# Two blocks of transformer layers on one core: other places for latents, forget steps, taps and first norms, a halved sub-norm reciprocal, and squares summed by TensorE

## The reference

```
first network                                      second network (twice)
h += attention(rms_norm(h))  # layer 0             y = rms_norm(x) @ w_in  -> four branches
h += conv_ffn(rms_norm(h))                          a: chunk band attention, 4 heads, relative bias
h += recurrent_mixer(rms_norm(h))  # layer 1        b: latents: rms_norm of 256 and 128 columns, up-projected
h += conv_ffn(rms_norm(h))                             to 4 heads, rotary part, chunk causal attention
attention: 8 heads of dilated mixture,              c: 4 heads, causal, logits + cumulated log forget gates
  and 4 differential heads:                         d: u = value * sigmoid(gate); causal depthwise convolution
  o = (softmax_1 - lam * softmax_2) @ v                over 31 taps; layer norm; silu
  o = rms_norm(o, b_sub_norm) * 0.8                x += sum_n(sigmoid(gate_n) * (branch_n @ w_branch_n)) @ w_o
                                                   x += relu(rms_norm(x) @ w_up)^2 @ w_down
                                                   at the end: rms_norm(x)
```

## Time and profile before

| | us |
|---|---|
| median of three runs | 2975.66 |
| the profiled execution, its own time | 2974.41 |
| its span | 2972.6 |
| PE busy | 2828.2 (95%) |
| DVE busy | 1354.6 (46%) |
| ACT busy | 1209.6 (41%) |
| POOL busy | 1244.1 (42%) |
| mean granted TensorE clock | 0.976 of full |

### The profile page before, as it was taken

How to read it: one execution, slowest core, us unless ns; L and a number is a source line. 1 busy time by engine, 2 the same in 40 slices (tenths; PEclk the granted TensorE clock), 3 DMA queues, 4 the chain that set the end, 5 groups by cost and what they waited for, 6 DMA issues and landing times.

```text
span 2972.6 us, 32386 instructions
## 1 busy us (share of the span) xinstructions
PE 2828.2 (95%) x12934; PEld 2286.1 (77%) x12934; DVE 1354.6 (46%) x2094; ACT 1209.6 (41%) x1781; POOL 1244.1 (42%) x550
## 2 busy tenths in 40 slices
PE   8998999999879999997899999999978999999997
PEld 7775788888757888875677788888756777888886
DVE  4565651545875415436456552022245566531113
ACT  3554442444544424334364444233244644342331
POOL 3212344444553444431257544444422466444442
PEclk9998999999999999998999999999989999999999
DMA  4211233232212332331122232332221222333322
GB/s 143 80 60 54 74 97 106 93 100 92 79 64 92 100 98 94 100 93 56 58 71 92 85 99 93 99 99 94 98 71 58 64 83 89 98 96 96 99 96 74
DMA packets 73926, 259.21 MB, mean 87 GB/s; under 512 B 9184, under 2 KB 9184, under 8 KB 73776
## 3 DMA queue, kind: packets, MB, share of 16 engines
q1 hardware_dynamic: 71680, 251.79, 26.6%
q10 hardware_dynamic: 2096, 5.36, 0.5%
HBM read 254.95 MB, written 2.13 MB: 86 GB/s over the span
## 4 chain that ended last, share of the span: by engine, by line
PE 86%; DVE 6%; ACT 3%; issue 2%; POOL 1%; DMA 1%; SPq 0%; DVEq 0%; ACTq 0%; POOLq 0%
PE ps L418 25%; PE ps L420 25%; PE ps L419 25%; PE ps L482 3%; PE ps L512 2%; PE ps L537 1%; PE ps L495 1%; PE ps L539 1%; PE ps L538 1%; POOL w_lo L1837 1%; PE ps L427 1%; PE ps L464 1%; PE ps L465 1%; PE ps L466 1%; ACT w_hi L855 0%
## 5 line engine op out<-in xcount | busy, mean ns | idle before, releaser
L1837 POOL TENSOR_TENSOR w_lo<-raw,w_hi 128x1024 fp32r<-128x1024 f32 x470 | 1142.5, 2433 | 1620.5 <-ACT w_hi L855 1620.2
L418 PE MATMUL ps<-xs,w_hi 128*128 128x512 f32 x2176 | 865.0, 398 | 17.0 <-POOL w_lo L1837 10.1
L419 PE MATMUL ps<-xs,w_hi 128*128 128x512 f32 x2176 | 850.6, 391 | 0.0
L420 PE MATMUL ps<-xs,w_lo 128*128 128x512 f32 x2176 | 850.5, 391 | 0.0
L855 ACT ACTIVATE w_hi<-raw 128x1024 fp32r<-128x1024 f32 x470 | 493.9, 1052 | 653.8 <-PE ps L420 606.0
L418 PE MATMUL ps<-hid,w_hi 128*128 128x512 f32 x1320 | 523.9, 397 | 56.0 <-issue 22.8
L419 PE MATMUL ps<-hid,w_hi 128*128 128x512 f32 x1320 | 519.5, 394 | 0.0
L420 PE MATMUL ps<-hid,w_lo 128*128 128x512 f32 x1320 | 519.4, 393 | 0.0
L418 PEld LDWEIGHTS ps<-xs,w_hi 128*128 128x128 f32 x2176 | 411.0, 189 | 119.6 <-issue 13.0
L419 PEld LDWEIGHTS ps<-xs,w_hi 128*128 128x128 f32 x2176 | 411.2, 189 | 88.5 <-issue 4.4
L420 PEld LDWEIGHTS ps<-xs,w_lo 128*128 128x128 f32 x2176 | 410.6, 189 | 86.7
(11 more groups left out here) (208 smaller groups left out, 2650.1 us busy)
## 6 DMA issues: line engine op xcount, KB each, us to landing
raw<-in_weights SPq DMA_DIRECT2D x470, 512.0 KB, 3.4
hT<-in_x ACTq DMA_DIRECT2D x4, 512.0 KB, 9.5
btab<-in_rel SPq DMA_DIRECT2D x8, 256.0 KB, 3.8
out<-tmp ACTq DMA_DIRECT2D x8, 256.0 KB, 2.4
btab<-in_heads SPq DMA_DIRECT2D x6, 256.0 KB, 3.8
tmp<-in_heads SPq DMA_DIRECT2D x6, 256.0 KB, 4.2
common<-in_fixed ACTq DMA_DIRECT2D x1, 642.0 KB, 13.1
small<-in_small ACTq DMA_DIRECT2D x1, 368.5 KB, 4.6
```

The lines of the kernel that those rows point to most:

```text
L418: pe.matmul(banks[bank][:], wh, rh, start=(k == 0), stop=False)
L419: pe.matmul(banks[bank][:], wh, rl, start=False, stop=False)
L420: last = pe.matmul(banks[bank][:], wl, rh, start=False, stop=(k == len(specs) - 1))
L1837: gp.tensor_tensor(w_lo[:, n % NPAIR, :], raw[:, n % NRAW, :], w_hi[:, n % NPAIR, :].bitcast(F32), ALU.subtract).then_inc(*w_low.tick(n))
```

## The change

It moves steps, gives steps other banks, splits one reciprocal in two, and hands one sum to PE.

- In a block, steps beside it now come ahead of the due sub-norm steps.
- The sub-norm has three steps: submean, subrec (first 256 columns of the reciprocal) and subnorm (the other 256, the product, the low part). Its sum has bank 3; the turns of the differential units all use bank 2.
- The pairs of the first attention have other banks, and the first two pairs' turns stand behind the next unit. The out steps have other banks and places, with one more chunk set (output 7) ahead of the last norm.
- In the second network the latents start in block 0, two d_input steps stand between rope and the first b_key, the forget steps start behind block 4 (8 before), 44 taps stand in blocks 10 to 25 (26 in 16 to 25), and 12 gated steps (10).
- For the norm behind the attention (m = 1) DVE adds no squares; PE sums each chunk's square into bank 7 between the chunks of the first up linear, and ACT's square of chunk c waits for the sum of chunk c - 3.

```diff
@@ attention_steps
+                steps += beside.get(n, [])
                 steps += due
-                steps += beside.get(n, [])
@@
-            return [("submean", u), ("subnorm", u)] if stage == "first" and u >= 4 else []
+            return [("submean", u), ("subrec", u), ("subnorm", u)] if stage == "first" and u >= 4 else []
-            return 2 + ((k + n) % 2 if is_lam(stage, n // NB) else k)
+            return 2 + k
-        pair_banks = [((5, 6), (7, 5), (6, 7))[p % 3] for p in range(8)]
-        vb_banks = {(0, 0): 5, (0, 1): 6, (1, 0): 6, (1, 1): 5}
+        pair_banks = [(5, 6), (7, 2)] + [((5, 6), (7, 5), (6, 7))[p % 3] for p in range(6)]
+        vb_banks = {(0, 0): 7, (0, 1): 6, (1, 0): 5, (1, 1): 6}
         for p in range(2):
-            before0 += [f for part in behind_next(p, unit_steps(p + 1)) for f in part]
+            after = unit_steps(p + 1)
+            before0 += after[:1] + [("qk_root", p), ("qk_norm", p)] + after[1:] + [("qk_turn", p)]
-        beside0[25], beside0[26] = last_vb[2:3], last_vb[3:]
-        out_banks = (5, 6, 0, 1, 2, 3, 4, 7)
-        early0 = {27: [(0, 0, 4)], 28: [(1, 0, 4)], 29: [(0, 4, 5), (1, 4, 5)], 30: [(0, 5, 6), (1, 5, 6)], 32: [(2, 0, 4)],
-                  33: [(3, 0, 4), (0, 6, 7), (1, 6, 7)], 34: [(2, 4, 7), (3, 4, 7)], 35: [(4, 0, 7), (5, 0, 7)]}
+        beside0[24], beside0[25] = last_vb[2:3], last_vb[3:]
+        out_banks = (5, 6, 7, 0, 1, 2, 4, 3)
+        early0 = {26: [(0, 0, 4)], 27: [(1, 0, 4)], 28: [(0, 4, 5), (1, 4, 5)], 29: [(2, 0, 5)],
+                  30: [(0, 5, 6), (1, 5, 6), (2, 5, 6)], 32: [(3, 0, 5)], 33: [(4, 0, 5)],
+                  34: [(0, 6, 7), (1, 6, 7), (2, 6, 7), (3, 5, 7), (4, 5, 7)], 35: [(5, 0, 7)], 36: [(7, 0, 7)]}
@@ second network
-        beside2 = {0: [("latent", 0)], 1: [("latent", 1)], 2: [("latent", 2)], 3: [("latent_norms", 0), ("rope", 0)],
-                   4: [("latent_parts", 1), ("b_key", 0), ("b_key", 1)], 5: [("latent_parts", 0), ("b_values", 0)],
-                   6: [("b_query", 0), ("b_query", 1)], 7: [("b_key", 2), ("b_key", 3)], 8: [("b_query", 2), ("b_query", 3)],
-                   9: [("d_input", (0, 0))], 10: [("d_input", (0, 1))], 11: [("c_head", 4)], 12: [("c_head", 6)],
-                   13: [("d_input", (1, 0))], 14: [("d_input", (1, 1))], 15: [("c_head", 5)], 16: [("c_head", 7)],
-                   25: [("gated", (1, 0)), ("gated", (1, 1))]}
-        for c in range(8):
-            beside2[17 + c] = [("gated", (0, c))]
+        beside2 = {0: [("latent", 0), ("latent", 1)], 1: [("latent", 2)], 2: [("latent_norms", 0), ("rope", 0)],
+                   3: [("latent_parts", 1), ("d_input", (0, 0))], 4: [("latent_parts", 0), ("d_input", (0, 1))],
+                   5: [("b_key", 0), ("b_key", 1), ("b_values", 0), ("b_query", 0)],
+                   6: [("b_query", 1), ("b_key", 2), ("b_key", 3)], 7: [("d_input", (1, 0))], 8: [("d_input", (1, 1))],
+                   9: [("b_query", 2), ("b_query", 3)], 10: [("c_head", 4)], 11: [("c_head", 6)], 12: [("gated", (0, 0))],
+                   13: [("c_head", 5)], 14: [("c_head", 7)]}
+        for n, g in enumerate([(0, c) for c in range(1, 8)] + [(1, c) for c in range(4)]):
+            beside2[15 + n] = [("gated", g)]
-                behind2.setdefault(8 + i * 8 // len(forget), []).append(("forget", f))
-        for i, f in enumerate(tap_list[:26]):
-            behind2.setdefault(16 + i * 10 // 26, []).append(f)
+                behind2.setdefault(4 + i * 8 // len(forget), []).append(("forget", f))
+        for i, f in enumerate(tap_list[:44]):
+            behind2.setdefault(10 + i * 16 // 44, []).append(f)
-        for i, (n, c) in enumerate([(1, c) for c in range(2, 8)] + [(2, c) for c in range(5)]):
-            steps2 += rest[max(0, 4 * i - 8):max(0, 4 * i - 4)] + [("gated", (n, c))]
+        for i, (n, c) in enumerate([(1, c) for c in range(4, 8)] + [(2, c) for c in range(5)]):
+            steps2 += rest[2 * i:2 * i + 2] + [("gated", (n, c))]
@@ PE
-                    bk = 7
+                    bk = 3
-                out_first(o, 7 if o < 6 else 0, 8)
+                out_first(o, 0 if o == 6 else 7, 8)
+            def square_sum(k):
+                for c in [k - 1] if 0 < k < 7 else [6, 7] if k else []:
+                    T.wait_ge(squared, ("x", 1, c))
+                    if c == 0:
+                        wait_bank(7)
+                    t = pe.matmul(banks[7][:], one1024, tmp[:, c % 3, :], start=(c == 0), stop=(c == 7))
+                    t.then_inc(*mean.tick(*([("square", c)] + ([("root", 1)] if c == 7 else []))))
+                if k == 7:
+                    free[7] = (rooted, ("root", 1))
...
+                            linear(..., between=square_sum if first and m == 1 else None)
@@ ACT, square_chunk
+                if m == 1:
+                    A.wait_ge(mean, ("square", c - 3) if c > 2 else "tokens")
+                    ac.activation(tmp[:, c % 3, :], hT[:, c, :], ACT.Square).then_inc(*squared.tick(("x", m, c)))
@@ DVE
-                if c:
+                if c and m != 1:
+                elif what == "subrec":
+                    V.wait_ge(rooted, ("sub", a))
+                    chain(ve.reciprocal(tmp[:, 2, 0:256], tmp[:, 2, 0:256]))
                 elif what == "subnorm":
-                    chain(ve.reciprocal(b, b))
+                    chain(ve.reciprocal(b[:, 256:S], b[:, 256:S]))
```

More of the change, by code:

```diff
@@ L354, in program @@
             if f:
-                behind2.setdefault(8 + i * 8 // len(forget), []).append(("forget", f))
-        for i, f in enumerate(tap_list[:26]):
-            behind2.setdefault(16 + i * 10 // 26, []).append(f)
+                behind2.setdefault(4 + i * 8 // len(forget), []).append(("forget", f))
+        for i, f in enumerate(tap_list[:44]):
+            behind2.setdefault(10 + i * 16 // 44, []).append(f)
         steps2 = attention_steps("second", 6, beside2, behind2)
-        rest = tap_list[26:]
-        for i, (n, c) in enumerate([(1, c) for c in range(2, 8)] + [(2, c) for c in range(5)]):
-            steps2 += rest[max(0, 4 * i - 8):max(0, 4 * i - 4)] + [("gated", (n, c))]
+        rest = tap_list[44:]
+        for i, (n, c) in enumerate([(1, c) for c in range(4, 8)] + [(2, c) for c in range(5)]):
+            steps2 += rest[2 * i:2 * i + 2] + [("gated", (n, c))]
         steps2 += [("conv_mean", 0), ("gated", (2, 5)), ("conv_var", 0), ("gated", (2, 6)), ("conv_norm", 0), ("gated", (2, 7)),
@@ L400, in wait_bank, with linear @@
                     T.wait_ge(*free[bank])
-            def linear(bank, group, specs, rhs, operand, k0=0, k1=None):
+            def linear(bank, group, specs, rhs, operand, k0=0, k1=None, between=None):
                 k1 = len(specs) if k1 is None else k1
@@ L423, in linear @@
                         last.then_inc(*product.tick(*done))
+                    if between:
+                        between(k)
             def sum_over(bank, event, lhs, rhs):
@@ L624, in tensor @@
                     out_first(*a)
-            for c, o in enumerate(range(8)):
-                out_first(o, 7 if o < 6 else 0, 8)
+            for o in range(8):
+                out_first(o, 0 if o == 6 else 7, 8)
                 free[out_banks[o]] = (resid, ("attn", o))
+            def square_sum(k):
[7 more added lines that the diff above has]
+                    free[7] = (rooted, ("root", 1))
             def network(L, m):
@@ L634, in network @@
                             bank = (2 * c + half) % 6
-                            linear(bank, ("up", L, c, half), mat("ffn_w_up", L, P * (c + 24 * half)), xr, x_chunk(m))
+                            first = c == 0 and half == 0
+                            linear(bank, ("up", L, c, half), mat("ffn_w_up", L, P * (c + 24 * half)), xr, x_chunk(m),
+                                   between=square_sum if first and m == 1 else None)
                             free[bank] = (taps, ("up", L, c, half))
-                            if c == 0 and half == 0:
+                            if first and m != 1:
                                 root(m)
@@ L882, in square_chunk @@
                     return
-                if c == 0:
+                if m == 1:
+                    A.wait_ge(mean, ("square", c - 3) if c > 2 else "tokens")
+                    ac.activation(tmp[:, c % 3, :], hT[:, c, :], ACT.Square).then_inc(*squared.tick(("x", m, c)))
+                elif c == 0:
                     if m:
@@ L1008, in scalar @@
                         A.wait_ge(low, ("y", "first", a - 1))
-                    ac.activation(tmp[:, 2, :], banks[7][:], ACT.Sqrt, bias=eps,
+                    ac.activation(tmp[:, 2, :], banks[3][:], ACT.Sqrt, bias=eps,
                                   scale=1.0).then_inc(*rooted.tick(("sub", a)))
@@ L1465, in vector @@
                         take_low(y["first", a], banks[4][:], ("y", "first", a))
+                elif what == "subrec":
+                    V.wait_ge(rooted, ("sub", a))
```

(4 more changed lines are left out.)

## The result

The changed kernel takes 2932.34 us (median of 4 runs, 2926.04 to 2934.66) beside 2976.12 us for the kernel before on the same chip: ratio 0.9849, 95% interval 0.9831 to 0.9867, 44 us faster. The forecast was 2929.5. The profiled execution took 2934.61 us, 39.8 us less than the one before.

The account below looks back on a forecast made before the run. PE was taken as the bound, with time to gain only in its idle waits and low clock, mostly in the attention stages. Savings summing to 45.9 us from 2974.4 gave 2928.5, stated as 2929.5 on the median's scale; range 2917 to 2941.

Parts of the forecast that it names:

- Part 1: Second network's forget steps: starting four blocks earlier removes aug's DMA wait and its clock, 21.4 us, less 2.6 at f3.
- Part 2: Second network's latents: two d_input linears cover part of the wait; about 9 us at b_key 1 remain, 12.0 saved.
- Rival A: Second network's latents fully covered, DVE through d(0,1) before PE reaches b_key 1: 28.6 us less, 2901; chance 0.10.
- Part 3: Taps in the second network's attention blocks, 44 instead of 26: zero gain, between -3 and +10 us.
- Part 4: First attention's sub-norm and its bank: four waits of PE removed or shortened, each judged separately.
- (a): First attention, qk_turn 7: separate banks end the 3.6 us wait for the sub-norm's root, leaving 0.45 us.
- (c): First attention, y6: more out chunks ahead remove its 2.9 us wait; 0.7 us of a mix wait stays.
- (b): First attention, reciprocal halved over two blocks: the 3.3 us wait goes, the 3.8 us one becomes about 1.4 at y5.
- (d): First attention, y7: ACT's conversion of the next slab, not the norm, sets the wait; 3.5 us remain.
- Part 5: Norm behind the first attention: PE's seven more sums cost 6.0 us, with 3 us idle in the up linear.
- Part 6: First pairs in the prelude: moving pair 1's turn behind the unit saves 2.2 us, between 0 and 5.
- B: Waits only move: DVE's two-input operations meet POOL's w_lo and the latents save nothing; 2940 to 2950, chance 0.18.

Follow-up runs that it names:

- u_forget: The changed kernel with the forget steps back behind blocks 8 to 15: 2950.89 us, ratio 0.9913 to the kernel before.
- s_swap: The changed kernel with d_input (0, 1) ahead of latent_parts 0 in block 4 of the second network: 2934.23 us, ratio 0.985.
- x_lat2: The changed kernel with the second network's d_input halves and c_head 4 ahead of latent_parts 0, b products from block 7: 2927.35 us, ratio 0.9837.
- u_taps: The changed kernel with 26 taps in blocks 16 to 25 again and four per gated step behind: 2934.13 us, ratio 0.9856.
- u_squares: The changed kernel with DVE again adding the squares of the norm behind the attention, one sum on PE: 2929.78 us, ratio 0.984.
- x_tab: The changed kernel with the first network's first bias tables requested right behind the slabs of unit (1, 0, 0): 2923.59 us, ratio 0.9822.

## Why the prediction was right

- **Idle time.** The terms together put PE's idle time down by 34.7 us; it fell by 34.3. By stage the gaps fell by 1.8, 8.8, 11.5 and 10.9 us in the prelude, the first attention and the two layers, where the terms hold 2.2, 10.4, 11.1 and 11.1, and by 1.3 us in stages that the change does not touch: the close total is in part luck.
- **Low clock.** The terms put its cost down by 17.2 us; the profiled executions leave 39.8 - 34.3 + 6.0 = 11.5. So of the 6.1 us by which the profile falls short of the forecast 5.7 are clock. The first attention gave 8.0 of 8.6; layer 0 gave 3.6 of 4.8 and layer 1 1.4 of 3.8; and between the first attention and the second network 2.3 us were lost with fewer gaps, where nothing was changed. The term that was mis-sized is the clock of the second network. The median (43.8 us off) fell short by 2.1 only, which is within what the four runs spread.
- **Part 1** held: no wait for aug, and u_forget brings it back. The low level behind aug's wait was rightly read: in the trace of before it lasts 5.8 and 5.3 us behind the two waits, 2.9 and 2.6 us lost for the 2.6 taken. The price at f3 is a wait of 0.98 us per layer (1.3 charged).
- **Part 2** held in mechanism, and its size with some luck (see the collision below): 9.07 us at b_key 1 for L1736 (9 forecast) and 1.40 at b_values for L1720 (2 forecast), in both layers. PE's timeline: start, us, engine, line, operation, idle before and its releaser:

```profile
1377.27 0.79 PE L420 MATMUL ps<-hid,w_hi 128*128 128x512 f32 x1 [9.07 <-DVE att L1736]
...
1381.60 0.58 PE L770 MATMUL ps<-w_hi,hid 128*128 128x256 f32 x1 [1.40 <-DVE att L1720]
```

  The low level behind it lasts 9.6 us in layer 0 and 7.6 in layer 1, 1.4 of each idle, so it costs 4.1 and 3.1 us where 3 were charged. Rival A needed DVE to reach d (0, 1) before the latents, and s_swap shows that even this only hands the wait on. x_lat2 shows that the order can buy a few us, and not the 14 per layer that A supposed.
- **The collision left out of the sum did come.** The bias tables met POOL's conversion in both layers. DVE's and PE's timelines, then POOL's:

```profile
1362.62 3.47 DVE L1805 SCALAR_TENSOR_TENSOR tmp<-btab,common 128x512 f32<-128x512 f32 x2
...
1366.35 0.96 PE L486 MATMUL ps<-att 64*128 64x256 f32 x4 [1.01 <-DVE tiny L1355]
```

```profile
1363.00 2.53 POOL L1859 TENSOR_TENSOR w_lo<-raw,w_hi 128x1024 fp32r<-128x1024 f32 x1 [12.14 <-ACT w_hi L872]
```

  3.47 us for a pair that took 1.29 in the trace of before (the line L1783 there), so 2.2 us late, and 1.0 us of it shows as a wait at score 5; the other 1.2 lie inside the 9.07. The walk gave 9 without any collision, so it was about 1 us too long elsewhere, and the two errors met by luck (an estimate; no run has these latents without the collision). The sum with the collision, 2934, is as near to the measured 2932.3 as the one without. What the same trace shows of operations with one of their operands in PSUM: L1328 has a mean of 697 ns over 182 records, L1316 687 over 96, none stretched, though 116 of them overlap an operation of POOL. L1297 with both inputs in SBUF has 1745: the 41 of its 64 records that overlap one of POOL's have a mean of 2304, and none of the other 23 took over 753. The Trainium skill, "SBUF — State Buffer", section "SBUF: two separate sides", restricts the lock in just this way, to DVE operations with two SBUF inputs or in a 2-port mode. By that rule, the trace agrees. One case more: a scale of pbuf with a single SBUF input was held too, 1.41 us for 0.29; whether it counts among the operations in a 2-port mode no run here tells.
- **Part 3**: zero, shown by u_taps within its interval.
- **Part 4**: (a) and (c) held (no wait for the root, 0.7 us at the mix). (b) was mis-sized, 3.2 us for 1.4. The walk had the reciprocal halved in the right blocks, but DVE's weigh stood under POOL's conversion (233.66 to 236.06) for 1.41 us, where the same line takes 0.29 undisturbed (its shortest of 16). That put the second half 1.1 us back; the other 0.7 us is not placed. (d) 3.49 for 3.5. DVE's timeline:

```profile
234.74 1.41 DVE L1375 TENSOR_SCALAR pbuf<-pbuf,tiny 128x128 f32<-128x128 f32 x1
...
236.77 1.75 DVE L1491 RECIPROCAL tmp<-tmp 128x256 f32<-128x256 f32 x1
```

- **Part 5** held: idle gaps of 1.55, 0.32, 0.32 and 1.33 us in the first up linears for 3, and a collision of 2.33 us on one chunk. u_squares speaks for the edit as such costing some 2.6 us, though that lies within what the intervals leave open: PE's 6 us of sums buy 2.6 us of idle time. DVE's and PE's timelines:

```profile
298.33 2.33 DVE L1297 SCALAR_TENSOR_TENSOR xs<-hT,small,xs 128x512 fp32r<-128x512 f32 x1 [1.16 <-ACT xs L896]
...
300.72 0.50 PE L420 MATMUL ps<-xs,w_hi 128*128 128x512 f32 x1 [1.55 <-DVE xs L1297]
```

- **Part 6**: 2.3 for 2.2 us, which one execution cannot tell so closely: u_forget, with the same instructions there, is 4.4 us ahead at that point. The gaps of the prelude fell by 1.8 us. The wait for the table stayed, 4.2 for 5.1, and x_tab shows what it was worth.

Rivals B (2940 and more), C and D are out: the pieces B named came in part (2.2 us at the tables twice, 1.8 at y 5), the taps bind nothing, and the first attention alone gave 10.8 us, so more than aug's wait went.

What stays open: the four runs of the changed kernel spread over 8.6 us. The trace of u_forget, whose program is the same up to the second network, is 3.3 us ahead by the end of the first attention with the same gaps within 0.2 us; its granted clock from 45 to 325 us is 0.98 for 0.96, so the difference comes from where the low stretches fall. What sets that was not tried.

## What to carry to other kernels

Before work is put beside a long chain on another engine, write down that engine's queue: a product whose bank has to be freed behind the chain covers nothing, and moving one step only hands the wait to the next taker of a bank. Count a long idle stretch of TensorE together with the low clock behind it (here waits of 3.5 and 4.2 us were worth 5.2 and 7.8 by the stages of the traces). Where such a wait went altogether the clock came back with it; where one was shortened from 9.1 to 3.7 us it did not. With one edit of the latter kind that is a hint and no rule. Before a gain of a few us is laid to an edit, see in which stage it lies. The cheapest gains here were two requests that stood one place too late in a queue: a table's DMA behind slabs, and a conversion ahead of the high part that was waited for.

## What the runs showed of the hardware

- The granted clock of 0.50 lasted about as long behind 3.7 us of idle time (9.0 and 6.8 us) as behind 9.1 (9.6 and 7.6). In the first attention of the changed kernel it lasted 6.0 us behind a single idle of 3.2 us and 3.4 us behind one of 3.5. Taking away idles of 4.2 and 3.5 us gave 7.8 and 5.2 us in their stages.
- Shorter idles had it too: 3.4 us at 0.50 came behind 1.6 us of idle time at 107 us and behind 1.8 us at 1287 us. In u_forget the same 1.6 us idle, at 106 us, is followed by 1.00.
- Identical instructions with gaps alike within 0.2 us differed by 3.3 us between two executions, through the placing of the low stretches. Differences of that size between variants of this kernel need several runs of each, and here even medians of four leave them open.
- DVE operations with both inputs in SBUF were held beside POOL, and only there: L1297 took 2.30 us in the mean of the 41 that overlap an operation of POOL, and at most 0.75 in the other 23. None of the 278 operations L1328 and L1316, with one input in PSUM, took over 0.70 us, 116 of them beside POOL.
- A reciprocal on DVE takes 3.35 us for 128x512 and 1.74 us for 128x256, where products and differences of 128x512 take 0.69 to 0.75.
